# Attention and retention scores: heads of two row halves side by side

## The reference, cut to what matters

```python
# retention: 8 heads, dk = 64, chunks of 128 tokens
scores = jnp.einsum('bnchd,bnmhd->bnhcm', qc, kc) * decay
inner  = jnp.einsum('bnhcm,bnmhe->bnche', scores, vc)
# attention: 16 query heads, 4 key heads, width 64, blocks of 128 queries, window 128
s = jnp.einsum('bnqhgd,bnkhd->bnhgqk', qb, kk)        # kk: the block before and this one
s = jnp.where(valid, s, NEG_INF)
m = jnp.maximum(jnp.max(s, -1), sink)
p = jnp.exp(s - m); p = p / (sum(p) + jnp.exp(sink - m))
o = jnp.einsum('bnhgqk,bnkhd->bnqhgd', p, vv)
```

## Time and profile before

| | before |
|---|---|
| median of 3 runs | 2291.95 us (2290.33 to 2292.55) |
| the profiled execution | 2291.22 us, span 2289.4 us, granted clock 0.99 |
| PE busy | 2178.3 us, 95% of the span |
| PEld busy | 2000.7 us, 87% |
| DVE busy | 1655.0 us, 72% |
| ACT busy | 1182.8 us, 52% |
| POOL busy | 398.3 us, 17% |
| DMA | 409.77 MB, mean 179 GB/s |

### The profile page before, as it was taken

The page is one execution under the profiler, slowest core; times in us unless marked ns, Lnnn a source line. Parts: engine busy times, 40 slices in busy tenths (PEclk is TensorE's granted clock), DMA queues, the critical chain, the costliest instruction groups (busy, mean ns, idle before and its releaser), DMA issues.

```text
span 2289.4 us, 42454 instructions
## 1 busy us (share of the span) xinstructions
PE 2178.3 (95%) x14844; PEld 2000.7 (87%) x14844; DVE 1655.0 (72%) x2970; ACT 1182.8 (52%) x2051; POOL 398.3 (17%) x324
## 2 busy tenths in 40 slices
PE   3999999999999999999989999999999999999998
PEld 2988989999899978888888898999999998888886
DVE  7887657999777677887664666499987776666665
ACT  3346545544666544544454474454456665444444
POOL 0000000000699800000000000000009994000000
PEclk7999999999999999999999999999999999999999
DMA  7854544555433378887543334455553333555553
GB/s 296 294 212 149 174 149 153 181 181 184 138 112 118 117 254 292 287 292 254 193 169 120 120 121 166 157 183 182 180 172 120 111 111 131 193 193 193 193 193 124
DMA packets 112002, 409.77 MB, mean 179 GB/s; under 512 B 12432, under 2 KB 12944, under 8 KB 111248
## 3 DMA queue, kind: packets, MB, share of 16 engines
q1 hardware_dynamic: 111888, 408.24, 52.6%
HBM read 406.62 MB, written 1.57 MB: 178 GB/s over the span
## 4 chain that ended last, share of the span: by engine, by line
PE 76%; POOL 16%; DVE 3%; ACT 3%; issue 1%; DMA 0%; SPq 0%; ACTq 0%; DVEq 0%
PE ps L1331 31%; POOL hot L368 16%; PE ps L1048 12%; PE ps L1052 12%; PE ps L1049 12%; PE ps L1261 1%; PE ps L1192 1%; PE ps L1100 1%; DVE w_lo L618 1%; PE ps L1294 1%; ACT w_hi L382 1%; PE ps L1118 1%; DVE big L691 1%; DVE big L670 1%; PE ps L1310 1%
## 5 line engine op out<-in xcount | busy, mean ns | idle before, releaser
L618 DVE TENSOR_TENSOR w_lo<-raw,w_hi 128x1024 fp32r<-128x1024 f32 x664 | 814.3, 1227 | 315.1 <-ACT w_hi L382 293.2
L382 ACT CAST w_hi<-raw 128x1024 fp32r<-128x1024 f32 x664 | 694.8, 1046 | 665.4 <-PE ps L1052 600.0
L1048 PE MATMUL ps<-h_hi,w_hi 128*128 128x256 f32 x3072 | 769.3, 288 | 1.8 <-ACT big L387 1.6
L1049 PE MATMUL ps<-h_lo,w_hi 128*128 128x256 f32 x3072 | 753.7, 283 | 0.0
L368 POOL TENSOR_SCALAR hot<-con,rt 128x128 f32<-128x128 f32 x320 | 398.1, 1257 | 1513.6 <-DVE neg L984 1513.6
L1048 PEld LDWEIGHTS ps<-h_hi,w_hi 128*128 128x128 f32 x3072 | 589.0, 192 | 16.1 <-ACT w_hi L382 7.9
L1049 PEld LDWEIGHTS ps<-h_lo,w_hi 128*128 128x128 f32 x3072 | 589.6, 192 | 0.9 <-issue 0.5
L1052 PE MATMUL ps<-h_hi,w_lo 128*128 128x256 f32 x3072 | 431.3, 283 | 0.4 <-DVE w_lo L618 0.4
L1052 PEld LDWEIGHTS ps<-h_hi,w_lo 128*128 128x128 f32 x3072 | 396.2, 192 | 1.1 <-DVE w_lo L618 0.8
L582 ACT CAST p_hi<-big 128x256 fp32r (+1 forms) x256 | 103.8, 406 | 350.4 <-PE ps L1331 349.3
L1331 PE MATMUL ps<-w_hi,p_hi 128*128 128x512 f32 x1024 | 276.2, 391 | 5.2 <-ACT p_hi L582 5.0
(11 more groups left out here) (175 smaller groups left out, 1585.1 us busy)
## 6 DMA issues: line engine op xcount, KB each, us to landing
raw<-in_u SPq DMA_DIRECT2D x256, 512.0 KB, 3.4
raw<-in_v SPq DMA_DIRECT2D x256, 512.0 KB, 3.6
raw<-in_win SPq DMA_DIRECT2D x104, 512.0 KB, 4.1
hot<-in_ada SPq DMA_DIRECT2D x80, 512.0 KB, 3.6
raw<-in_wq SPq DMA_DIRECT2D x32, 512.0 KB, 4.2
big<-in_ada SPq DMA_DIRECT2D x16, 512.0 KB, 14.7
raw<-in_wout SPq DMA_DIRECT2D x16, 512.0 KB, 3.6
big<-in_decay SPq DMA_DIRECT2D x2, 1536.0 KB, 12.1
```

Source lines behind the costliest of these rows:

```text
L382: nc.scalar.copy(w_hi[:, j % 2, :], raw[:, j, :]).then_inc(hi_ready, 1)
L618: tt(w_lo[:, j % 2, :], raw[:, j, :], w_hi[:, j % 2, :].bitcast(F32), ALU.subtract).then_inc(lo_ready, 1)
L1048: mm(o, w, h_hi[:, k, :], start=(k == 0), stop=False)
L1049: mm(o, w, h_lo[:, k, :], start=False, stop=False)
```

## The change

`score_heads(j)` pairs the attention heads anew, as (0, 1), (4, 5), (2, 3), (6, 7), (8, 9), (12, 13), (10, 11), (14, 15); bank 4 + j % 2 gets pair j, so that bank 4 holds heads of the lower row half and bank 5 of the upper. `att_score(b, i)` makes four heads, two per bank, and issues them alternating between the halves; it waits until all masks of the visit before are done, and both pairs' semaphore counts come from the last two matmuls. `ret_score(i)` makes both heads of a pair behind one block, 10, 12, 14 and 16, first the 256-wide matmuls of the two halves, then the 128-wide ones; it waits until both heads of the pair before are decayed. VectorE's pieces stay behind their blocks.

```diff
@@ -97,6 +97,12 @@
 G_FIRST = N_U1 + 4
 M_PROD = N_U1 + 5
 N_PROD = N_U - M_PROD
+
+
+def score_heads(j):
+
+    h = 8 * (j // 4) + 4 * (j % 2) + 2 * (j // 2 % 2)
+    return h, h + 1
 
 
 def gate_after(b):
@@ -760,9 +766,9 @@
                     w = P * (b + 1)
                     q = TB * l + b
                     dve.wait_ge(att_scored, 8 * q + j + 1)
-                    for h in (2 * j, 2 * j + 1):
+                    for a, h in enumerate(score_heads(j)):
                         last = nc.vector.tensor_tensor_reduce(
-                            s_att[b][:, h, 0:w], bank(4 + j % 2)[:, 2 * P * (h % 2):2 * P * (h % 2) + w],
+                            s_att[b][:, h, 0:w], bank(4 + j % 2)[:, 2 * P * a:2 * P * a + w],
                             mask_t[:, 2 * P - w:2 * P], ATT_SCALE, sink[:, h:h + 1], ALU.add, ALU.max,
                             small[:, b, 0, h:h + 1])
                     last.then_inc(att_masked, 1)
@@ -1130,15 +1136,17 @@
                                         pj[:, c + a, P * t:P * (t + 1)], ident)
                     last.then_inc(v_turned, 1)
 
-                def ret_score(h):
-                    pe.wait_ge(rotated, N_ROT * l + (3 if h < 4 else 4))
-                    if h >= 2:
-                        pe.wait_ge(ret_decayed, RH * l + h - 1)
-                    r = slice(RDK * (h % 2), RDK * (h % 2 + 1))
-                    q_, k_ = pj[r, C_RQ + h // 2, :], pj[r, C_RK + h // 2, :]
-                    o = bank(4 + h % 2)
-                    mm(o[:, 0:SEQ], k_[:, 0:P], q_, start=True, stop=True)
-                    mm(o[:, SEQ:DW], k_[:, P:SEQ], q_[:, P:SEQ], start=True, stop=True).then_inc(ret_scored, 1)
+                def ret_score(i):
+                    pe.wait_ge(rotated, N_ROT * l + (3 if i < 2 else 4))
+                    if i:
+                        pe.wait_ge(ret_decayed, RH * l + 2 * i)
+                    q_, k_ = pj[:, C_RQ + i, :], pj[:, C_RK + i, :]
+                    half = [slice(RDK * a, RDK * (a + 1)) for a in range(2)]
+                    for a in range(2):
+                        mm(bank(4 + a)[:, 0:SEQ], k_[half[a], 0:P], q_[half[a], :], start=True, stop=True)
+                    for a in range(2):
+                        mm(bank(4 + a)[:, SEQ:DW], k_[half[a], P:SEQ], q_[half[a], P:SEQ], start=True, stop=True
+                           ).then_inc(ret_scored, 1)
 
                 def ret_sum(g):
                     pe.wait_ge(v_copied, 5 * l + g + 1)
@@ -1176,21 +1184,24 @@
                     mm(bank(6 + g % 2), ident[0:4, g:g + 1].broadcast_to([4, P]), stat, start=True, stop=True
                        ).then_inc(gn_spread, 1)
 
-                def att_score(b, j):
+                def att_score(b, i):
                     w = P * (b + 1)
                     q = TB * l + b
-                    if b == 0 and j == 0:
+                    if b == 0 and i == 0:
                         pe.wait_ge(rotated, N_ROT * (l + 1))
                         pe.wait_ge(gn_std, l + 1)
-                    if b or j >= 2:
-                        pe.wait_ge(att_masked, 8 * q + j - 1)
-                    for h in (2 * j, 2 * j + 1):
-                        kv = h // (AH // AKV)
-                        r = slice(AHD * (kv % 2), AHD * (kv % 2 + 1))
-                        aq = pj[r, C_AQ + 4 * (kv // 2) + h % 4, P * b:P * (b + 1)]
-                        ak = pj[r, C_AK + kv // 2, SEQ - 2 * P:w]
-                        last = mm(bank(4 + j % 2)[:, 2 * P * (h % 2):2 * P * (h % 2) + w], aq, ak, start=True, stop=True)
-                    last.then_inc(att_scored, 1)
+                    if b or i:
+                        pe.wait_ge(att_masked, 8 * q + 2 * i)
+                    for j in range(2):
+                        for a in range(2):
+                            h = score_heads(2 * i + a)[j]
+                            kv = h // (AH // AKV)
+                            r = slice(AHD * (kv % 2), AHD * (kv % 2 + 1))
+                            aq = pj[r, C_AQ + 4 * (kv // 2) + h % 4, P * b:P * (b + 1)]
+                            ak = pj[r, C_AK + kv // 2, SEQ - 2 * P:w]
+                            last = mm(bank(4 + a)[:, 2 * P * j:2 * P * j + w], aq, ak, start=True, stop=True)
+                            if j:
+                                last.then_inc(att_scored, 1)
 
                 def turn_p(b, g):
                     hs = 4 // (b + 1)
@@ -1222,8 +1233,8 @@
                     project(l * N_BLOCKS + m, l * EV + m, m % RING)
                     if m in (3, 5, 7, 9):
                         swap((m - 3) // 2)
-                    if 10 <= m < 18:
-                        ret_score(m - 10)
+                    if m in (10, 12, 14, 16):
+                        ret_score((m - 10) // 2)
                     if m in (11, 13, 15, 17, 29):
                         turn_v((m - 11) // 2 if m < 29 else 4)
                     if m in (13, 15, 17, 19):
@@ -1237,8 +1248,7 @@
                     if 28 <= m < 32:
                         spread(m - 28)
                     if 29 <= m < 37:
-                        for j in (0, 1):
-                            att_score((m - 29) // 4, 2 * ((m - 29) % 4) + j)
+                        att_score((m - 29) // 4, (m - 29) % 4)
                     if 35 <= m < 39:
                         turn_p(0, m - 35)
                     if 39 <= m < 43:
```

## The result

| | before | after |
|---|---|---|
| median | 2291.69 us (4 runs, 2290.33 to 2292.55) | 2274.12 us (4 runs, 2272.84 to 2274.80) |
| ratio | | 0.9923, 95% interval 0.9906 to 0.9940 |
| span of the profiled execution | 2289.4 us | 2272.9 us |
| PE busy | 2178.3 us | 2162.5 us |
| DVE busy | 1655.0 us | 1654.1 us |

The kernel is 17.6 us faster (by the interval 13.8 to 21.5); forecast were 18.3 less than before, as 2273.5 us. The bytes moved (409.77 MB) and the number of matmuls (14844) are the same.

The account below looks back on a forecast made before the run. The prediction took TensorE's time as the kernel's time in the changed stages. Gains of 7.9 (retention), 3.5 and 6.9 us (attention b = 0, b = 1) sum to 18.3, giving 2273.5 us, range 2272.0 to 2279.5.

Parts of the forecast that it names:

- Overlap of row halves: Retention and attention scores: loads and matmuls of two row halves run doubled, as att_sum's column halves do; chance 0.68.
- R3: Rival: row halves don't overlap; only the saved entering and leaving of visits remains, 2.7 us, time 2289.3; chance 0.06.
- R4: Rival: no overlap and every change of half costs 0.19 us; 11.0 us slower, 2303; chance 0.05.
- R2: Rival: matmuls of the halves overlap, loads don't; gain 13.0 us, time 2279.0; chance 0.17 together with R1.
- Retention: Visits behind blocks 11, 13, 15, 17 go, 0.99 us each; those left cost the same; 7.9 us over two layers.
- the stronger waits: Visits wait for both heads or all four masks of the one before: retention 0.6 us spare, cost 0; VectorE just keeps up.
- Attention: Score visits shrink by 0.44 us for b = 0 and 0.86 for b = 1; 3.5 and 6.9 us in all.
- R1: Rival: matmuls start in program order, so each visit keeps one slot more; gain 14.0 us, 2278.0; chance 0.17 with R2.
- near 0: Sign in the profile after: VectorE's idle time before the attention masks falls to about nothing.
- the 4.09 against 4.12: Attention, b = 1: VectorE needs 4.09 us a block with masks, probs and w_lo; TensorE's beat falls to 4.12.
- The thin cover: Layer 0, visit behind late weight block 32: 0.3 us spare, cost taken as 0, at most 1.8 us lost.
- The sum: Retention 7.9, attention b = 0 3.5 and b = 1 6.9: 18.3 us gained over both layers.

Follow-up runs that it names:

- e3: Changed kernel with both heads of each visit in one row half, same visits, waits and bank alternation: 2289.1 us, ratio 0.9988 to the kernel before.
- e1: Only retention's part of the change, attention as in the kernel before: 2284.7 us, ratio 0.9971.
- e2: Only the attention's part of the change, retention as in the kernel before: 2281.1 us, ratio 0.9954.
- e4: Changed kernel with each visit's matmuls reordered, all of the lower row half first, then all of the upper: 2273.8 us, ratio 0.9924.
- e10: Changed kernel with layer 0's weight block 32 issued one DMA earlier and b = 0 in two eight-head visits, on the third chip: 2273.7 us, ratio 0.9918.
- e9: The changed kernel again, unaltered, on the third chip: 2271.8 us, ratio 0.9911.
- e7: Changed kernel with b = 0 in two eight-head visits, issued lower half first, then upper: 2275.3 us in its one run.
- e6: Changed kernel with b = 0 attention scores in two visits of eight heads, halves alternating: 2273.6 us, ratio 0.9915.

## Why the prediction was right

*Overlap of row halves.* The step that I took from another shape, full doubling, held: loads and matmuls both (two loads in 0.19 us, two matmuls at once), and e3 shows that little else carries the gain (2.9 of 17.6 us). R3 and R4 fall; so does R2, since the 128-wide visit, where loads fill the time, shrank from 1.16 to 0.72 us.

*Retention.* Forecast 0.99 us a removed visit and no change in those left: blocks 11, 13, 15, 17 lost 0.99 to 1.00 in both layers, 10 and 14 stayed at 3.91. In e1 by itself 7.3 us by the medians against 7.9. Layer 0's block 12 is the exception, see the stronger waits.

*Attention.* Forecast 0.44 and 0.86 a block; measured in layer 1 0.43 to 0.45 and 0.85 to 0.87. By itself 10.9 us against 10.4 (e2).

*Program order (R1).* It gave 14.0 us and fell: a 256-wide block took 4.13, where R1 had 4.33. And e4 says more than att_sum could: the order inside a short visit doesn't matter. The Trainium skill's rule in "TensorE: Matmul & The Clock Gate", Part 3 (The mechanism), that matmuls start strictly in program order, does not hold here for different row halves: by the pair at 187.39 and e4's ratio the measurement decides.

*The stronger waits.* For retention the forecast was 0.6 us spare and cost 0. That holds in layer 1, but in layer 0 the changed kernel paid 0.12 us. These are VectorE's piece for head 1 and the visit behind block 12, which now waits for it:

```profile
91.65 0.56 DVE L747 TENSOR_TENSOR big<-ps,big 128x384 f32<-128x384 f32 x1
...
92.35 0.70 PE L1146 MATMUL ps<-big 64*128 64x256 f32 x4
```

The visit began 1.16 us behind the start of its block (91.19), not 1.05, and the block took 4.03, not 3.91. VectorE's piece came 0.74 later than before (90.91), and VectorE was late by as much at 82.91, ahead of the first edited piece; so the lateness is not from the change, but the old wait, for head 0 alone, would not have passed it on. In e10 the same block took 3.95, in e1 and e4 to e9 3.91 or 3.92. Attention, b = 1: 0; turn_p's block 37 took 3.34, not 3.31, within the 0 to 0.1 forecast. VectorE's idle before a 256-wide mask went from 12.5 to 6.5 us over both layers, not to near 0 as I wrote: blocks 33 and 34 still leave it 1.3 to 1.5 us each, and it catches up to TensorE only when probs joins, as the 4.09 against 4.12 said.

*The thin cover.* This is the step that missed by most. I had 0.3 us spare behind block 32 of layer 0 on the assumption that VectorE's chain would keep its distance to block 29. It came 0.75 later: weight block 32 took 5.82 us from issue (169.12) to ScalarE's start (174.94), against 5.07 before (172.84 to 177.91), 4.42 in e9 (168.40 to 172.82), 5.60 in e4 (where the visit waited 0.2) and 4.24 in e2. 0.3 less 0.75 is about the 0.48 that was waited. The issue time followed VectorE as assumed; the landing time is no constant, and a cover of 0.3 us under a DMA that swings by more than 1 us is none.

*The sum.* By the beats, layer 1 gained 9.1 us, half of 18.3 (9.15). Layer 0 gained 8.2: 0.5 less for block 32, and 0.4 and 0.1 that blocks 4 and 12 took longer. Block 4 stands ahead of any edit, and in e4 and e9 it took 2.9 again, so that is the execution's own swing; block 12 is the stronger wait above. The two mixers make 17.3, and the profiled spans differ by 16.5: stages without any edit took 0.7 us longer in this execution. In e9, the same kernel again, the mixers gained 9.6 and 9.1, and the medians differ by 20.7 (2292.44 to 2271.79). So the mechanism and the beats were forecast; that the first median came within 0.7 us of the forecast is in part luck, since the same change measured 17.6 and 20.7.

## What to carry to other kernels

A small matmul with 64 rows costs its columns and, if its neighbours have another shape, some 0.2 us for each change of shape. Put two such matmuls of different row halves, into different banks, in one visit: the pair costs what one did; here they could stand in any order as long as no more than three waited in between. Where TensorE sets the time, the beats of bare blocks and of blocks with one piece behind them give the price of each piece to 0.01 us, and a forecast made of them held to 0.1 us in layer 1; a transfer's landing time should enter such a sum as a range, and so should the time of any engine that waits for transfers.

## What the runs showed of the hardware

- Row halves overlap like column halves, for f32 operands in their two-pass form, loads included: 0.215 us for two 256-wide matmuls at once, e3's twin without it 0.215 each.
- A matmul for a free half passes three earlier ones that wait for the other half (e4: x8 in 1.14 us), and in e7 no more: with eight of the lower half in front, the first of the upper began beside the fifth (x16 in 1.71 us, alternating 1.16).
- The rest of 0.38 us around a 64-row visit: beside a 4-row matmul one visit less saves 0.20 besides the pitches, alone 0.39 (e6).
- The same 512 KB weight block took 4.24 to 5.82 us from its issue to ScalarE's start where ScalarE waited for it (e2, e9, before, e4, the change; one execution each).
- Not tried: two halves into one bank.
